# A decoder layer with PEER experts: gates by one 256-column matmul a token, one-hots shared out anew

## What is computed

```python
experts = jnp.take_along_axis(cand_idx, top_j, axis=-1).reshape(T, PEER_HEADS * PEER_TOPK)
gate = jax.nn.softmax(top_s.astype(jnp.float32), axis=-1).reshape(T, PEER_HEADS * PEER_TOPK)
...
u = expert_u[ec]
a = jax.nn.gelu(jnp.einsum('cd,ced->ce', xc, u).astype(jnp.float32), approximate=False)
return jnp.einsum('ce,ced->cd', (gc * a).astype(x.dtype), expert_v[ec])
```

## Time and profile before

| | |
|---|---|
| median of 3 runs | 1032.9 us (1032.48 to 1033.08) |
| profiled execution, device time | 1032.03 us |
| its span, first to last instruction | 1030.0 us |
| granted TensorE clock, mean | 0.998 |
| TensorE busy | 1016.0 us (99%) |
| VectorE busy | 742.2 us (72%) |
| ScalarE busy | 432.2 us (42%) |
| GpSimd busy | 107.1 us (10%) |

### The profile page before, as it was taken

One profiled execution on the slowest core, in us unless ns is written; L12 is line 12 of the kernel. 1 busy time (PEld: TensorE's weight loads), 2 busy tenths in 40 slices (PEclk: granted clock), 3 DMA queues, 4 the chain that ended last, 5 costly groups with the idle time before them and its releaser, 6 DMA issues.

```text
span 1030.0 us, 17462 instructions
## 1 busy us (share of the span) xinstructions
PE 1016.0 (99%) x6514; PEld 894.2 (87%) x6514; DVE 742.2 (72%) x1798; ACT 432.2 (42%) x763; POOL 107.1 (10%) x210
## 2 busy tenths in 40 slices
PE   9999999999999999999999999999999999999996
PEld 3478865999999999999999999988888888888885
DVE  1165543788999679999999975566666666666667
ACT  1245432233444755555555544443333334343441
POOL 1000000004000143333333300000000000000000
PEclk9999999999999999999999999999999999999999
DMA  9742200793555544444444455576555555555551
GB/s 334 308 162 105 83 21 0 223 343 122 183 182 182 179 155 136 141 144 144 143 136 138 139 164 184 185 245 214 195 193 196 190 197 188 200 188 200 187 181 42
DMA packets 48755, 176.52 MB, mean 171 GB/s; under 512 B 5136, under 2 KB 6176, under 8 KB 47520
## 3 DMA queue, kind: packets, MB, share of 16 engines
q1 hardware_dynamic: 48272, 173.82, 49.5%
q0 software_dynamic: 400, 1.58, 0.4%
HBM read 174.33 MB, written 1.05 MB: 170 GB/s over the span
## 4 chain that ended last, share of the span: by engine, by line
PE 97%; DVE 1%; DMA 1%; ACT 0%; SPq 0%; issue 0%; DVEq 0%
PE ps L464 95%; PE ps L643 1%; DMA arena<-in_w_tok 1%; DVE xs L1676 0%; DVE xs L1670 0%; DVE arena L1664 0%; DVE xs L1661 0%; PE ps L683 0%; PE ps L543 0%; PE ps L712 0%; PE ps L532 0%; ACT slab L973 0%; ACT arena L969 0%; SPq L358 0%; PE ps L847 0%
## 5 line engine op out<-in xcount | busy, mean ns | idle before, releaser
L464 PE MATMUL ps<-x1hl,hi 128*128 128x256 f32 x2216 | 377.7, 285 | 0.0
L464 PEld LDWEIGHTS ps<-x1hl,hi 128*128 128x128 f32 x2216 | 327.3, 192 | 0.0
L464 PE MATMUL ps<-hi,ahl 128*128 128x512 f32 x992 | 265.3, 389 | 0.0
L1114 ACT CAST hi<-slab 128x1024 fp32r<-128x1024 f32 x128 | 135.2, 1056 | 204.6 <-PE ps L464 204.4
L464 PEld LDWEIGHTS ps<-hi,ahl 128*128 128x128 f32 x992 | 186.2, 188 | 38.6
L464 PE MATMUL ps<-x1hl,lo 128*128 128x256 f32 x688 | 194.6, 283 | 0.0
L1626 DVE TENSOR_TENSOR lo<-slab,hi 128x1024 fp32r<-128x1024 f32 x128 | 156.0, 1219 | 0.0
L464 PE MATMUL ps<-lo,ahl 128*128 128x512 f32 x496 | 152.7, 389 | 0.0
L464 PEld LDWEIGHTS ps<-x1hl,lo 128*128 128x128 f32 x688 | 131.7, 191 | 0.0
L1405 DVE TENSOR_TENSOR lo<-slab,hi 128x1024 fp32r<-128x1024 f32 x86 | 106.1, 1233 | 16.3 <-ACT hi L1001 16.2
L464 PE MATMUL ps<-arena 128*128 128x128 f32 (+6 forms) x806 | 111.6, 293 | 1.9 <-DVE arena L1156 1.4
(11 more groups left out here) (201 smaller groups left out, 822.9 us busy)
## 6 DMA issues: line engine op xcount, KB each, us to landing
slab<-in_pv SPq DMA_DIRECT2D x128, 512.0 KB, 3.3
slab<-in_uT SPq DMA_DIRECT2D x107, 512.0 KB, 3.3
arena<-in_wq SPq DMA_DIRECT2D x32, 512.0 KB, 5.7
ahl_raw<-in_uT SPq DMA_DIRECT2D x21, 512.0 KB, 3.3
arena<-in_w_tok SPq DMA_DIRECT2D x2, 2048.0 KB, 16.7
arena<-in_w_out SPq DMA_DIRECT2D x1, 4096.0 KB, 13.3
arena<-in_w_tok SPq DMA_DIRECT2D x4, 512.0 KB, 8.3
arena<-in_w_tok SPq DMA_DIRECT2D x1, 1792.0 KB, 19.0
```

The source lines that it names most:

```text
L464: return nc.tensor.matmul(o, lhsT, rhs, start=start, stop=stop, skip_group_check=True)
L1114: nc.scalar.copy(hi[:, v_hi_slot(c), :], raw[:, v_slot(c), :]).then_inc(v_hi, 1)
```

## The change

The gate of a token becomes one fp32r matmul of 256 columns. Its moving operand `pair` is [onehot(i) x rest of gate | onehot(i) x high part of gate], 128 columns each; its stationary operand `hot2` is onehot(j). Low and high results lie side by side in PSUM, in two banks a group, in three sets (`GB` = 3), and are added afterwards: ScalarE's `save_low` copies the low half to SBUF, VectorE adds the high half to it.

Who makes the one-hots: VectorE both halves for tokens 0 and 1 (four two-scalar operations); GpSimd the plain onehot(i) for tokens 2 and 3 (`POOL_FIRST`), which ScalarE scales by the two gate parts (four Copy activations with a scalar operand); of the four onehot(j) GpSimd makes all or, in even groups, three, and ScalarE the other (`ACT_HOT`). So GpSimd makes 5 or 6, 5.5 in the mean.

Groups stand further apart: group g is before block 41 + floor(21 g / 16), the last before block 123; most intervals are one block, five of sixteen are two. The arena isn't filled with ones any more: `gate_group` writes the gates to the blocks that are still to come and multiplies those that are done, and a gelu is split between `gel` (tokens whose gate is there) and the arena (the others). The u ring goes from 6 to 5 buffers.

```diff
-UR, UH = 6, 3
+UR, UH = 5, 3
-GB = 4
+GB = 3
+DVE_PAIR, ACT_PAIR = (0, 1), (2, 3)
+POOL_FIRST = (2, 3)
+ACT_HOT = ((0,), ())
+GROUP_AT = [N0 + g * 21 // 16 for g in range(GN)]
...
@@ gpsimd
-            nc.gpsimd.memset(arena[:, N0 * S:A_S1], 1.0)
...
             def onehots(g):
-                nc.gpsimd.tensor_copy(n2[:, g % 2, :], slotT[:, 1, 4 * g:4 * g + 4]).then_inc(n2_ready, 1)
                 if g >= 2:
                     pool.wait_ge(pe_g, g - 1)
-                pool.wait_ge(n2_ready, g + 1)
-                for q in range(POOL_HOT):
-                    ins = nc.gpsimd.tensor_scalar(hot(g)[:, 0, q, :], iota, n2[:, g % 2, q:q + 1], None, ALU.is_equal)
-                ins.then_inc(oh2_ready, 1)
+                for q in POOL_FIRST:
+                    ins = nc.gpsimd.tensor_scalar(pair[:, g % 2, q, 1, :], iota, tbl[:, 4 * g + q, 0:1], None, ALU.is_equal)
+                    if q == POOL_FIRST[-1]:
+                        ins.then_inc(pool_first, 1)
+                for q in [q for q in range(4) if q not in ACT_HOT[g % len(ACT_HOT)]]:
+                    ins = nc.gpsimd.tensor_scalar(hot2[:, g % 2, q, :], iota, tbl[:, 4 * g + q, 1:2], None, ALU.is_equal)
+                ins.then_inc(pool_hot, 1)
@@ tensor
             def gates(g):
...
                 for q in range(4):
-                    last = mm(ps[:, gate_bank(g), q * P:(q + 1) * P], hot(g)[:, 0, q, :], hot(g)[:, 1, q, :],
-                              q == 0, True)
+                    last = mm(banks[:, q // 2, (q % 2) * S:(q % 2 + 1) * S], hot2[:, g % 2, q, :],
+                              pair[:, g % 2, q, :, :].rearrange("p a n -> p (a n)"), q % 2 == 0, True)
@@ scalar
+            def pairs(g):
+                if g >= 2:
+                    act.wait_ge(pe_g, g - 1)
...
+                for o, code in hots:
+                    nc.scalar.activation(o, iota, ACT.Abs, scale=-1.0, bias=code).then_inc(act_dist, 1)
+                act.wait_ge(pool_first, g + 1)
+                for q in ACT_PAIR:
+                    nc.scalar.activation(pair[:, g % 2, q, 0, :], pair[:, g % 2, q, 1, :].bitcast(F32), ACT.Copy,
+                                         scale=tbl[:, 4 * g + q, 2:3]).then_inc(act_lows, 1)
...
+            def save_low(g):
+                act.wait_ge(pe_g, g + 1)
+                if g >= 2:
+                    act.wait_ge(pre_gated, g - 1)
+                nc.scalar.copy(low[:, g % 2], ps[:, gate_banks(g), :].rearrange("p b (q a c) -> p a c (b q)", q=2, a=2)[:, 0]
+                               ).then_inc(low_saved, 1)
...
             for c in range(NK):
                 gelu(c)
-                if c + UH < NK:
-                    u_split(c + UH)
...
+                for g in range(GN):
+                    if GROUP_AT[g] == c + 1:
+                        save_low(g)
+                for g in range(1, GN):
+                    if GROUP_AT[g] == c + 2:
+                        pairs(g)
+                if c + UH < NK:
+                    u_split(c + UH)
@@ vector
+            def tables():
+                dve.wait_ge(rT_saved, T)
+                did(v.tensor_copy(tbl[:, :, 3].bitcast(F32R), tbl[:, :, 2]))
+                settle()
+                v.tensor_tensor(tbl[:, :, 2], tbl[:, :, 2], tbl[:, :, 3], ALU.subtract).then_inc(table_ready, 1)
...
+            def gate_group(g):
+                k = GROUP_AT[g]
...
+                dve.wait_ge(low_saved, g + 1)
+                did(v.tensor_tensor(both_low[:, 0:k, :], high[:, 0:k, :], both_low[:, 0:k, :], ALU.add))
+                v.tensor_tensor(a[:, k:NK, :], high[:, k:NK, :], both_low[:, k:NK, :], ALU.add)
+                settle()
+                dve.wait_ge(gelu_done, k)
+                v.tensor_tensor(a[:, 0:k, :], both_low[:, 0:k, :], a[:, 0:k, :], ALU.mult).then_inc(pre_gated, 1)
```

More of the change, by code:

```diff
@@ L79 @@
         NLEAD = NCAND
[L83 removed]
+K_IOTA, K_ID, K_TRI, K_CB, K_FREQ = 0, 128, 256, 512, 512 + T * NC
 K_ALL = K_FREQ + 12
@@ L394, in _ @@
             sp.wait_ge(x1_ready, 2)
-            for c in (0, 1, 4, 5):
+            for c in (0, 1, 4):
                 load_u(c)
@@ L864, in _ @@
                     turn_routes()
-                if 0 <= c - N0 < GN:
-                    gates(c - N0)
+                for g in range(GN):
+                    if GROUP_AT[g] == c:
+                        gates(g)
                 expert_in(c)
@@ L1095, in onehot @@
                 if g >= 2:
                     act.wait_ge(pe_g, g - 1)
[L1097 to L1106, removed]
+                else:
+                    act.wait_ge(rT_saved, T)
@@ new lines, in pairs @@
+                hots = [(hot2[:, g % 2, q, :], tbl[:, 4 * g + q, 1:2]) for q in ACT_HOT[g % len(ACT_HOT)]]
+                before = sum(len(ACT_HOT[i % len(ACT_HOT)]) for i in range(g))
+                for o, code in hots:
[4 more added lines that the diff above has]
+                                         scale=tbl[:, 4 * g + q, 2:3]).then_inc(act_lows, 1)
@@ new lines, in pairs @@
+                for n, (o, code) in enumerate(hots):
+                    act.wait_ge(act_dist, before + n + 1)
+                    nc.scalar.activation(o, o.bitcast(F32), ACT.Relu, scale=-1.0, bias=1.0)
+                for n, q in enumerate(ACT_PAIR):
+                    act.wait_ge(act_lows, len(ACT_PAIR) * g + n + 1)
+                    ins = nc.scalar.activation(pair[:, g % 2, q, 1, :], pair[:, g % 2, q, 1, :].bitcast(F32), ACT.Copy,
+                                               scale=tbl[:, 4 * g + q, 3:4])
@@ L1602, in block_gate @@
-            def block_gate(c, groups):
-                dve.wait_ge(gelu_done, c + 1)
[L1604 to L1609, removed]
+                for q in DVE_PAIR:
+                    for part in range(2):
+                        ins = v.tensor_scalar(pair[:, g % 2, q, part, :], iota, tbl[:, 4 * g + q, 0:1],
+                                              tbl[:, 4 * g + q, 2 + part:3 + part], ALU.is_equal, ALU.mult)
@@ L1613, in _ @@
                 fill()
-            dve.wait_ge(rT_saved, T)
+            tables()
             onehots(0)
             fill()
[L1617 to L1623, removed]
+            fill()
+            assert filled[0] == N0 + 1
             def v_rest(c):
@@ L1641, in a_split @@
                 v.tensor_tensor(o[:, 1, :], a, o[:, 0, :].bitcast(F32), ALU.subtract).then_inc(a_lo, 1)
-            for c in range(N0 + GN - 2, NK):
+            for c in range(N0, NK + 1):
                 if filled[0] < NK:
                     fill()
[L1646 to L1649, removed]
+                for g in range(1, GN):
+                    if GROUP_AT[g] == c + 1:
+                        onehots(g)
+                for g in range(GN):
+                    if GROUP_AT[g] == c:
+                        gate_group(g)
+                if c > N0:
+                    block_gate(c - 1)
+                if NK - 2 <= c < NK:
+                    a_split(c - NK + 2)
+                    v_rest(c - NK + 2)
             for c in range(2, NK):
```

111 lines of the change are left out of this document (45 added, 66 removed).

## The result

The changed kernel takes 1016.63 us in the median of 4 runs (1016.22 to 1016.76), beside it the kernel before 1032.69 (1032.25 to 1033.08): ratio 0.9844, 95% interval 0.9827 to 0.9861, 16 us or 1.6% faster. Forecast were 1026 and a gain of 7. The direction was right and the time lies in the range of 1013 to 1031, but the gain is more than twice the one forecast.

A forecast was written before the change was run, and what follows sets the result against it. TensorE bounds the stage now, GpSimd next: 63 x 4.55 + 14.9 = 301.6 us against 307.4, -5.8, taken as -7; profiled 1032.03 to 1025, median 0.9 above, so 1026. Its own range 1013 to 1031, with rivals 1007 to 1043.

The forecast's parts named there:

- TensorE's part: Gate group on TensorE: four 0.12 us matmuls, 0.48 for 0.89; 26 us saved, floor 4.23 us a group if TensorE alone sets it.
- T: Mean time a gate group takes in the stage; break-even at 4.64 us, each 0.1 on it is 6.3 us.
- GpSimd as the next bound: Gate-group stage: GpSimd sets T, 63 x 4.55 + 14.9 = 301.6 us against 307.4; chance 0.42, for T from 4.33 to 4.61.
- GpSimd's 4.55 a group: GpSimd's sum: one-hots 3.17, fills 1.13, VectorE's one-hots 0.12, multiply and block gate 0.13; bounds 3.92 and 5.20.
- the head start: First groups: one-hots of two groups are ready before block 41, so -7 us is taken for -5.8.
- the 0.86 a fill: GpSimd's loss to one VectorE fill: middle of 0.57 to 1.15 us, x 1.31 = 1.13 a group.
- The multiply's term: GpSimd's loss to VectorE's new multiply and the block gate, two SBUF reads each: 0.13 us a group, bounds 0 and 0.4.
- Rival (1): TensorE stays the bound, a fill costing GpSimd under 0.7: T 4.23 to 4.33, 1007 to 1013 us; chance 0.22.
- Rival (2): Slower: fills block GpSimd at a higher price, deciding from a loss of 0.93; 1043 to 1062 us; chance 0.28.
- Rival (3): VectorE's 4.5 late sets T, or ScalarE's wait for GpSimd delays u splits: T near 4.4, 1018 us; chance 0.06.
- Rival (4): GpSimd, where first, holds VectorE for the rest of its one-hot: T = 5.5, +54, 1087 us; chance 0.02.
- The rest: Table's added VectorE operations, 5 u buffers, V's loads after the last group: together 0 us, bounds 0 and +3.

## Why the prediction was right and where it fell short

- **TensorE's part** held: 0.48 for a group, a floor of 4.23. With the fill's second read away T was 4.24.
- **GpSimd as the next bound** held: it is full between the groups, 27% of the chain, and half a one-hot more or less moves the time by +23 and -6 us.
- **The term that was mis-sized is GpSimd's 4.55 a group.** From its first one-hot (358.32) to the end of its last (642.09) its 64 groups take 283.8 us, 4.43 each. In parts: one-hots alone 3.17, as said; fills 66.4/64 = 1.04 against 1.13, since a fill costs 0.79 and not 0.86; all the rest 0.22 against 0.25. The difference, 0.116 x 64 = 7.4 us, is most of what the forecast of the stage was off (300.4 us from 365.20 forecast, 292.2 measured, 8.2). The remaining 0.8 is the head start, put at 1.2 us and worth about 2. Another 0.9 of the 9.4 us between 1026 and 1016.6 is what the forecast added from the profiled execution to the median; the changed kernel's profiled execution, 1016.70, lies at its median. T itself, 4.38, is inside the forecast's 4.33 to 4.61: the mechanism was right, its size was off.
- **The step that failed is the 0.86 a fill**, the middle of an even spread. The runs show that GpSimd's reads aren't spread evenly: 58 of 83 lose less than 0.76. They keep a phase to VectorE's work, and the same fills cost 0.79 each in the changed kernel and 0.94 with nothing moved but VectorE's one-hots. The changed kernel has one of the cheaper phases; nothing in the forecast or in the change aimed at it, so that part of the gain is luck. The forecast could bound the price (0.57 to 1.15) but not place it, and T moves by 1.31 times as much: from 0.79 to 0.94 that is 12 us. Its size can't be had from rows that show a fill met at one phase only.
- **The multiply's term** had the right size, 0.13 a group against 0.12 counted, but as an edit the wrong sign: without its second SBUF read the kernel was 4.6 us slower, since the fills' losses grew by 11.2 us. Terms of such a block can't be taken away one by one; they shift one another.
- **Rival (1)** asked for a fill under 0.7 by VectorE falling into step with GpSimd. Most reads do keep one place to the fill, but at 0.79, which is not enough for the floor, and not by the chain that it named: VectorE waited for `low` twice in the stage, 1.1 us in all. **Rival (2)** needed 0.93; merely putting VectorE's one-hots first brings 0.94 and a time within 1.2 us of the kernel before. **Rival (3)** gave 1018, nearer to the result than the forecast, by another cause than the one measured: no expert block of the stretch waited. VectorE's part of it is the bound that comes next, with 5 one-hots. **Rival (4)** fell: the longest hold-up of a fill by GpSimd in the changed kernel is 0.17 (1.39 for 1.22), not the rest of a 0.60 one-hot. The Trainium skill (SBUF — State Buffer, section Who interferes with whom) states that a VectorE instruction with two SBUF inputs contends with a GpSimd instruction that reads SBUF; taking one input of the fill away confirms it (286.2 to 219.8 us of one-hots).
- The rest (table, u ring of 5, late v loads) cost nothing that shows. The 1.2 us late start has another cause: a wait of ScalarE's for GpSimd with a u split queued behind. The prediction weighed that only for the steady state.
- Two of its sums don't close, and nothing hangs on them: by its terms GpSimd's lower bound is 3.17 + 0.75 + 0.12 = 4.04 and not 3.92, and the worst case of rival (2) is 3.17 + 1.51 + 0.12 + 0.40 = 5.20 and not 5.10 (1068 us, not 1062).

## What to carry to other kernels

When work moves to an engine that shares a port with another, count its instructions times their lone duration, add what the other engine's blocking instructions cost, and then treat that price as a range that the order of instructions decides: here it can be measured by moving one operand to PSUM. An engine that is full with an unlucky phase is best given less to do: here taking half a one-hot in 5.5 away brought 6.0 us, more than any reordering. Before a hand-over from one engine to another goes ahead of work that a third waits for, look at its first turn, where nobody has run ahead yet.

## What the hardware showed that was not expected

- A GpSimd one-hot of 0.60 us can be blocked in its first part only: it ends 0.39 or 0.47 us after the fill that blocked it, so what is left to do by then is less than the whole 0.60; and where it is first, the fill is held 0.17 us at most in the changed kernel.
- Of two VectorE instructions in a row with two SBUF inputs each, a waiting one-hot that started before the first was let in between them every time, one that started 0.04 us or more after it never, in the half fills and at the block gates of the changed kernel and of the run with the multiply from PSUM. In between both occur (let in at 0.02 in the changed kernel, held at 0.003 with the multiply from PSUM).
- Writing fp32r and taking the scalar from a strided table cost GpSimd nothing that shows: in the changed kernel the two of onehot(i) still take 1.18 where no fill is near (the 0.60 of the earlier trace rows twice, less the overlap).

```profile
367.31 1.18 POOL L443 TENSOR_SCALAR pair<-slab 128x128 fp32r<-128x128 f32 x2
```
